# Routing in a two-layer transformer kernel: remainders in four parts, bfloat16 counts, and the first expert's gate and up product between two halves of its gather

## What is computed

```python
h2 = modulate(rms_norm(x, norm2_g[i]), sh2, s2)
# route: probs = softmax(h2 @ router_w + router_b) in 4 groups of 8 experts;
#   the group with the largest sum of its two largest; in it the two largest: experts, gates = vals / sum(vals)
# each expert: (silu(xb @ w_gate[e]) * (xb @ w_up[e])) @ w_down[e], on the tokens sent to it
x = x + g2 * moe(...)          # sum over the two experts of a token, times their gates
```

## Time and profile before

| | |
|---|---|
| runs | 1302.55, 1303.06, 1304.62 us |
| the profiled execution | 1301.58 us, its span 1299.7 us |
| TensorE busy | 1191.6 us (92%) |
| VectorE / ScalarE / GpSimd busy | 453.3 / 178.3 / 73.2 us |
| moved | 485.50 MB, mean 374 GB/s |
| mean granted TensorE clock | 0.997 |

### The profile page before, as it was taken

The page is one execution under the profiler, slowest core; times in us unless marked ns, Lnnn a source line. Parts: engine busy times, 40 slices in busy tenths (PEclk is TensorE's granted clock), DMA queues, the critical chain, the costliest instruction groups (busy, mean ns, idle before and its releaser), DMA issues.

```text
span 1299.7 us, 13694 instructions
## 1 busy us (share of the span) xinstructions
PE 1191.6 (92%) x5006; PEld 491.7 (38%) x5008; DVE 453.3 (35%) x933; ACT 178.3 (14%) x375; POOL 73.2 (6%) x86
## 2 busy tenths in 40 slices
PE   6999999889999999999888899899999999988887
PEld 3444445544333333332222276443333333322222
DVE  4286776576211122111112156651112211121212
ACT  2212126522000000000000011310000000000000
POOL 0112100000000000000000000000000000000000
PEclk9999999999999999999999999999999999999999
DMA  9958759286999999999999997589999999999995
GB/s 352 398 206 345 259 205 402 95 344 263 423 422 421 422 422 422 422 422 422 422 422 421 419 406 306 229 344 421 422 422 423 421 422 422 422 422 422 422 422 245
DMA packets 80933, 485.50 MB, mean 374 GB/s; under 512 B 6146, under 2 KB 7682, under 8 KB 31748
## 3 DMA queue, kind: packets, MB, share of 16 engines
q1 hardware_dynamic: 79168, 481.91, 90.7%
q10 hardware_dynamic: 1732, 3.16, 0.7%
HBM read 484.00 MB, written 1.05 MB: 373 GB/s over the span
## 4 chain that ended last, share of the span: by engine, by line
PE 56%; SPq 29%; DMA 5%; DVE 4%; ACT 3%; issue 2%; POOL 0%; DVEq 0%; ACTq 0%; POOLq 0%
SPq L325 24%; PE PS L825 18%; PE PS L844 9%; PE PS L635 8%; SPq L330 5%; PE PS L852 4%; DMA ring<-in_moe_w_up 4%; PE PS L707 2%; PE PS L605 2%; PE PS L1021 2%; PE PS L996 2%; DVE TMP L1779 1%; PE PS L814 1%; PE PS L578 1%; PE PS L819 1%
## 5 line engine op out<-in xcount | busy, mean ns | idle before, releaser
L825 PE MATMUL PS<-ring,KQH 128*64 128x512 f32 x2048 | 456.0, 594 | 25.0 <-DMA ring<-in_moe_w_up 23.4
L844 PE MATMUL PS<-ring,KQH 128*64 128x512 f32 x1024 | 233.8, 598 | 44.0 <-DVE TMP L1779 26.8
L825 PEld LDWEIGHTS PS<-ring,KQH 128*64 128x64 f32 x2048 | 147.7, 137 | 322.0 <-issue 267.7
L1797 DVE TENSOR_TENSOR KQH<-KQH,PS 128x256 f32<-128x256 f32 x64 | 38.9, 608 | 417.1 <-ACT KQH L1229 417.1
L844 PEld LDWEIGHTS PS<-ring,KQH 128*64 128x64 f32 x1024 | 70.0, 136 | 166.5 <-issue 132.0
L852 PE MATMUL PS<-TMP,KQH 128*128 128x512 f32 x256 | 126.4, 617 | 1.6 <-DVE TMP L1779 1.6
L1229 ACT ACTIVATE KQH<-PS 128x256 f32<-128x256 f32 x62 | 23.8, 383 | 694.8 <-PE PS L825 694.8
L635 PE MATMUL PS<-ring,KQH 128*128 128x512 f32 x256 | 114.0, 593 | 0.0
L1779 DVE TENSOR_TENSOR TMP<-PS,KQH 64x512 f32<-64x512 f32 x64 | 44.1, 689 | 134.5 <-PE PS L844 113.2
L1779 DVE TENSOR_TENSOR TMP<-PS,TMP 64x512 f32<-64x512 f32 x64 | 44.1, 689 | 134.4 <-PE PS L844 113.2
L465 POOL COPY KQH<-KQH 128x512 f32 x62 | 38.0, 614 | 818.6 <-PE PS L825 757.8
(11 more groups left out here) (249 smaller groups left out, 769.7 us busy)
## 6 DMA issues: line engine op xcount, KB each, us to landing
ring<-in_moe_w_gate SPq DMA_DIRECT2D x128, 1024.0 KB, 25.6
ring<-in_moe_w_up SPq DMA_DIRECT2D x128, 1024.0 KB, 26.4
ring<-in_moe_w_down SPq DMA_DIRECT2D x64, 2048.0 KB, 27.4
ring<-in_ada_w SPq DMA_DIRECT2D x23, 2048.0 KB, 13.3
ring<-in_attn_w_in SPq DMA_DIRECT2D x2, 4096.0 KB, 12.7
ring<-in_attn_w_in SPq DMA_DIRECT2D x2, 2048.0 KB, 21.3
ring<-in_attn_w_out SPq DMA_DIRECT2D x1, 4096.0 KB, 24.0
ring<-in_pool_w_in SPq DMA_DIRECT2D x1, 4096.0 KB, 34.5
```

Of the source, the lines that this page charges most:

```text
L825: ins = mm(PS[64 * f:64 * f + 64, 4, :], xs[:, k, 0:SLOTS], gu_w[s][:, :, k, 256 * f:256 * f + 256], start=k == 0, stop=k == KC - 1)
L844: ins = mm(PS[64 * f:64 * f + 64, 6, :], lhs, dn_w[s][:, c, 512 * f:512 * f + 512], start=c == 0, stop=c == 3)
```

## The change

Four edits, all in the two stretches.

1. `low_parts` handles half of the width: four instructions of 512 elements instead of two of 1024. Chunks 0 to 3 of tile 0 stand ahead of `routing` as before; chunks 0 to 3 of tile 1, then chunks 4 to 7 of tiles 0 and 1, stand behind the first `pick`.
2. `chosen` and copies of the triangle and the ones are bfloat16, so the five counting products are bfloat16. GpSimd makes the copies at the start of the program. The values are small whole numbers, exact in bfloat16.
3. The four instructions for the gates move from `routing` to behind the second `pick`.
4. TensorE gathers chunks 0 to 3, then runs expert 0's `gate_up` of chunks 0 to 3 (each chunk behind its own eviction), then gathers chunks 4 to 7, then runs `gate_up` of chunks 4 to 7. Chunks 0 to 3 are all evicted by ScalarE, 4 to 7 all by VectorE. The gather's banks become 5, 6, 7, 3, since bank 4 now accumulates `gate_up`.

A branch of `ada_fin` that no block took (the `sel` product) is dropped too; its place among the constants holds the bfloat16 copies.

```diff
-            b = (6, 7, 3, 2)[k % 4] if half else 4 + k % 4
+            b = ((5, 6, 7, 3), (6, 7, 3, 2))[half][k % 4]
...
+            pool.wait_ge(const_in, 32)
+            nc.gpsimd.tensor_copy(count_w, const[:, C_TRI:C_TRI + 2 * P]).then_inc(pool_consts, 1)
...
+                pe.wait_ge(pool_consts, 2)
+                mm(PS[:, 3, 0:32], ones_b, chosen[:, 0, :], start=True, stop=False)
+                mm(PS[:, 3, 0:32], ones_b, chosen[:, 1, :], start=False, stop=True).then_inc(rt_cnt, 1)
...
-                pe.wait_ge(lo_ready, 2 * L.l + 2)
-                for k in range(KC):
-                    if k >= 4:
-                        pe.wait_ge((L.xs_v, L.xs_a)[k % 2], (k - 4) // 2 + 1)
-                        gather_high(0, k, 0)
-                        gather_low(0, k, 0)
-                        gather_high(0, k, 1)
+                pe.wait_ge(lo_ready, 4 * L.l + 2)
+                for k in range(4):
                     gather_low(0, k, 1).then_inc(L.xg_done, 1)
                 pe.wait_ge(L.gu_in[L.slot(0)], 32)
-                pe.wait_ge(L.xs_v, 4)
-                pe.wait_ge(L.xs_a, 4)
-                gate_up(L.slot(0), dense, range(4)).then_inc(L.gu_half, 1)
+                for k in range(4):
+                    pe.wait_ge(L.xs_a, k + 1)
+                    ins = gate_up(L.slot(0), dense, [k])
+                ins.then_inc(L.gu_half, 1)
+                pe.wait_ge(lo_ready, 4 * L.l + 4)
+                for k in range(4, KC):
+                    for t in range(NT):
+                        gather_high(0, k, t)
+                        ins = gather_low(0, k, t)
+                    ins.then_inc(L.xg_done, 1)
                 pe.wait_ge(L.gu2_in[L.slot(0)], 32)
-                gate_up(L.slot(0), dense, range(4, KC)).then_inc(L.gu_done, 1)
+                for k in range(4, KC):
+                    pe.wait_ge(L.xs_v, k - 3)
+                    ins = gate_up(L.slot(0), dense, [k])
+                ins.then_inc(L.gu_done, 1)
...
             def experts(L):
-                for k in range(1, KC, 2):
+                for k in range(4):
                     spread(L, 0, k)
...
-                low_parts(L, 1)
+                low_parts(L, 1, 0)
+                for t in range(NT):
+                    low_parts(L, t, 1)
                 link(V.tensor_scalar(dpos2, dpos, -float(HALF), None, ALU.add))
-                for k in range(0, KC, 2):
+                for k in range(4, KC):
                     spread_v(L, 0, k)
-                dve.wait_ge(L.xg_done, KC)
                 pick(L, dpos2)
+                gates()
                 positions(L)
```

More of the change, by code:

```diff
@@ L208, in t2 @@
             return ap.rearrange("p (t e) -> p t e", t=NT)
+        chosen = t2(rt(8, 32).bitcast(BF16))
+        tri_b, ones_b = count_w[:, 0:P], count_w[:, P:2 * P]
         acc_of |= {8: QT[:, 512:1536], 11: TMP[:, 1024:2048]}
@@ L532, in ada_fin @@
                         pe.wait_ge(mod_raw, 2 * n + (2 if i % 6 in SPREAD_PARTS else half + 1))
-                        if i % 6 in COL_PARTS:
-                            for k in range(4 * half, 4 * half + 4):
-                                ins = tr(PS[:, half, 128 * (k % 4):128 * (k % 4) + 128], by_column(i, modraw, k), ident)
-                        else:
-                            ins = mm(bank(half), sel, modraw[:, 512 * half:512 * half + 512], start=True, stop=True)
+                        for k in range(4 * half, 4 * half + 4):
+                            ins = tr(PS[:, half, 128 * (k % 4):128 * (k % 4) + 128], by_column(i, modraw, k), ident)
                 else:
@@ L1570, in mean_square, with low_parts @@
                 V.tensor_scalar(msn[:, t:t + 1], ssn[:, t:t + 1], 1.0 / D, EPS, ALU.mult, ALU.add).then_inc(ms_ready, 1)
-            def low_parts(L, t):
+            def low_parts(L, t, half):
                 dve.wait_ge(xn_ready, 2 * L.l + t + 1)
-                V.scalar_tensor_tensor(xlo[:, t, :].rearrange("p (k q) -> p k q", k=KC), x_cols[t], msn[:, t:t + 1],
-                                       xhi[:, t, :].rearrange("p (k q) -> p k q", k=KC), ALU.mult, ALU.subtract).then_inc(lo_ready, 1)
+                chunks, columns = slice(4 * half, 4 * half + 4), slice(512 * half, 512 * half + 512)
+                V.scalar_tensor_tensor(xlo[:, t, columns].rearrange("p (k q) -> p k q", k=4), x_cols[t][:, chunks, :], msn[:, t:t + 1],
+                                       xhi[:, t, columns].rearrange("p (k q) -> p k q", k=4), ALU.mult, ALU.subtract).then_inc(lo_ready, 1)
             def norm_part():
@@ L1615, in routing @@
                 pr, pm, t, oh1, oh2, srt = (t2(rt(i)) for i in range(6))
-                chosen, td = t2(rt(8)), t2(rt(9))
+                td = t2(rt(9))
                 sm = rt(10, 64)
-                mx, _, tm, v1, v2, v12 = (sm[:, 2 * i:2 * i + 2] for i in range(6))
+                mx, _, tm, v1, v2 = (sm[:, 2 * i:2 * i + 2] for i in range(5))
                 gs, gt = sm[:, 16:24].rearrange("p (t g) -> p t g", t=NT), sm[:, 24:32].rearrange("p (t g) -> p t g", t=NT)
@@ L1686, in routing, with gates @@
                 link(V.reduce_sum(dpos, dsel_all.rearrange("p (a e) -> p a e", e=NE), AX))
+            def gates():
+                v1, v2, v12 = (rt(10)[:, 2 * i:2 * i + 2] for i in range(3, 6))
+                link(V.tensor_tensor(v12, v1, v2, ALU.add))
+                link(V.reciprocal(v12, v12))
+                V.tensor_tensor(gate[:, 0:2], v1, v12, ALU.mult)
+                link(V.tensor_tensor(gate[:, 2:4], v2, v12, ALU.mult))
             dstart = rt(15)[:, 32:64]
```

28 lines of the change are left out of this document (10 added, 18 removed).

## The result

The changed kernel takes 1309.74 us (median of 5 runs, 1309.09 to 1310.54), the kernel before 1303.32 us beside it (5 runs, 1302.55 to 1304.62). The ratio is 1.0050, 95% interval 1.0039 to 1.0060: slower by 6.4 us. I had predicted 1312.8 us in a range of 1308 to 1317.5, so the sign, the place and the mechanism were right and the size was 3.1 us too high, for reasons given at the end.

A forecast was written before the change was run, and what follows sets the result against it. Expert-weight loads, set by when each may be issued, were taken to bound the loop. Per layer 3.35 us for late `h_ready` plus 1.5 us for the clock, 9.7 us over two layers, gave 1312.8 us; range 1308 to 1317.5.

The forecast's parts named there:

- The bound and the mechanism: Expert loop: loads bound it; VectorE's late row delays the down load, leaving the queue empty for over 6 us.
- The rival "faster": Down load follows TensorE, 1.55 us earlier, 1300.0 us; sign: `hidden` starts before about 308.5; chance 0.05.
- Gain 0; the GpSimd operation hides it: Before routing: the shorter remainder frees VectorE 1.05 us earlier, but L1628 still waits for GpSimd's inverse root; gain 0.
- Counts: Five counting products in bfloat16 on TensorE: 0.57 to 0.85 us saved, 0.55 taken.
- The clock in front: Expert 0's first gather: eight products at half clock, so the last products of chunks 0 to 3 start 0.65 us earlier.
- `h_ready` 3.35 us later: VectorE behind the late evictions of chunks 4 to 7: `h_ready` at 313.5 instead of 310.13, 3.35 us later.
- The clock behind: TensorE after its 4.9 us wait for `hidden`: half clock for transposes, gathers and start of `down`, 1.5 us a layer.
- the one gap that I took as evidence: TensorE idle 1.16 us, busy 1.75 of 2.90 us; granted clock then 0.50 from 292.9 to 296.2.
- The sum: A layer: 3.35 + 1.5 = 4.85 us; two layers: 9.7 us slower.
- the term for `hidden`: The 3.35 us a layer by which `h_ready`, and with it the down load, comes later.
- the case without the clock's fall: Clock stays up behind the wait: 3.35 twice, 1309.8 us, or 1308.3 with 0.65 more gained in front; chance 0.22.

The follow-up runs named there:

- moving that row away: Changed kernel with VectorE's `hidden` and second-half evictions placed ahead of most of the remaining routing: 1298.15 us, -5.4 us against the kernel before.
- Edits 2 and 3 alone: Kernel before plus only the bfloat16 counts and the gates behind the second pick: 1301.84 us, -1.9 us against the kernel before.
- edit 4 alone: Kernel before plus only the new TensorE and VectorE order around expert 0: 1313.63 us, +10.1 us against the kernel before.
- filling the wait: Changed kernel with four unused float32 products on TensorE ahead of its wait for `h_ready`: 1306.11 us, +2.6 us against the kernel before.

## Why the prediction came out as it did

- **The bound and the mechanism: right.** Loads bound the loop, the two early loads bring nothing, and the down load waits for VectorE's row behind the late evictions. The wait was 4.36 us (4.9 predicted), the DMA share 0.14 for ten microseconds (a queue empty for over 6 predicted), and moving that row away turned +6.4 us into -5.4. The rival "faster" fell by the point named for it: `hidden` started at 32.6 from the anchor, not at the 30.2 that its 308.5 means.
- **"Gain 0; the GpSimd operation hides it": wrong, 0.8 us a layer.** I took the inverse root's 2.27 us as its own length. It ends 0.37 us behind the remainder beside it in both kernels (before: 284.65 against 282.22 + 2.06; now: 286.20 against 285.83), and with the shorter remainder routing started 0.8 us earlier, at 5.64 instead of 6.44 us behind the anchor, now released by the router's product. The Trainium skill says why, in "SBUF — State Buffer", section on SBUF's two separate sides: VectorE and GpSimd share a pair of ports under an exclusive lock, held for the whole instruction, which a VectorE operation with two inputs in SBUF takes against a GpSimd operation that reads SBUF. L1583 is one, and the trace agrees (2.27, 1.34, 0.56 us). I should have weighed it.
- **Counts: 0.81 us instead of 0.55.** The five products start 0.03 us apart (292.84 to 292.96), less than the lower end that I had set (0.3 us for five). TensorE is through with them 1.0 us sooner; 0.81 of it reach VectorE, whose own two instructions on the counts then follow without a wait. Edits 2 and 3 alone show 0.8 us as well.
- **The clock in front: missed, about 0.9 us a layer.** I had put half clock under the gather, from the earlier trace rows. In the changed kernel it ran at full clock (1.00 from 290 to 302), 0.12 us a product, so the last products of chunks 0 to 3 came 2.5 us earlier instead of 0.65: 1.6 from the two points above, 0.9 behind the first gather product. Full clock alone would not have given that 0.9. In edits 2 and 3, at full clock, these products waited for tile 1's remainder and came 0.81 us earlier, no more than the gather; in edit 4 alone, at full clock too, they came at 18.88 us from the anchor, in the kernel before at 18.87. So edit 1's shorter remainder is needed for it. That it takes the full clock as well is worked out, not shown by a run: in the kernel before, the high products before them took until 297.17, 0.05 us longer than the remainder. `gate_up` started 5.45 us earlier instead of 3.44.
- **`h_ready` 3.35 us later: mis-sized, 1.33.** The working behind it held: evictions, pick, gates and a row of 7.8 us. It started from a gather that was 2.0 us too late, and that is the whole difference.
- **The clock behind: 1.5 us predicted, 1.93 and 1.54 measured** (7.87 and 7.48 less 5.94); filling the wait gave 1.90 and 1.52. In layer 1 it was the stretch of 3.3 us that I had priced. In layer 0 it lasted 6.6 us and cost little more only because 2.2 of them fell into the wait: there the size is luck. And the one gap that I took as evidence was thinner than it looked. In edit 4 alone, layer 0, TensorE did the same (an idle of 1.16 us, ten float32 passes, 1.74 of 2.90 us busy) and the clock stayed up:

```profile
291.53:294.43 2.90, 1.74 (x13) 1.50 (x13) 2.07 (x13) 0.00 (x0) 0.00 (x0) 1.00 1.00 418
294.43:297.73 3.30, 2.83 (x16) 1.76 (x14) 3.20 (x8) 0.00 (x0) 0.00 (x0) 1.00 0.83 345
```

- **The sum.** 4.85 us a layer predicted, 3.26 and 2.88 measured. The three errors in front (0.8, 0.26 and 0.9) are 2.0 us a layer in one direction; the clock behind gave 0.4 back in layer 0. That makes 3.6 us in all by the traces, 3.1 by the medians. So the term for `hidden` was 2.5 times too large (3.35 against 1.33), and the range held because it was wide enough for that. A slip in the range: with the 0.55 more that was left to gain in front, the case without the clock's fall is 1308.7 us, not 1308.3; the range stays as it was.

## What to carry to other kernels

Where a queue is the bound, write down the waits of all its entries, and ask of each change which is the last one that finds the queue empty; an earlier first entry is worth nothing until the later ones follow, and moving one ahead soon makes the next the limit. Before work is moved earlier on one engine, look at what the engine that feeds the last wait still has queued, and put what nobody waits for behind it. Don't read the length of an operation as its own where it always ends with an operation of another engine beside it.
